# One block from the convolution to the ffn, with single waits in place of two block ends

## The reference

```python
mod = silu(c) @ w_ada + b_ada                      # sh1, sc1, g1, sh2, sc2, g2
h = x * (1 + sc1) + sh1
z, xbc, dt_raw, q, k, v, f_raw = split(h @ w_in)
xbc = silu(causal_depthwise_conv(xbc, conv_w, conv_b))
y_ssm = rms_norm((ssd_chunked(xs, dt, A, Bm, Cm) + d_skip * xs) * silu(z))
y_att = rms_norm(forgetting_attention(q, k, v, log_f))
x = layer_norm(ALPHA * x + (1 + g1) * (concat(y_ssm, y_att) @ w_out))
h = x * (1 + sc2) + sh2
x = layer_norm(ALPHA * x + (1 + g2) * (square(relu(h @ w_ff_in)) @ w_ff_out))
```

## Time and profile before

| what | us |
|---|---|
| median of 3 runs (2339.7 to 2341.65) | 2341.12 |
| profiled execution | 2340.7 |
| its span, first to last instruction | 2338.9 |
| TensorE busy | 2243.1 |
| VectorE busy | 869.9 |
| ScalarE busy | 646.1 |
| GpSimd busy | 335.7 |

### The profile page before, as it was taken

How to read it: one execution, slowest core, us unless ns; L and a number is a source line. 1 busy time by engine, 2 the same in 40 slices (tenths; PEclk the granted TensorE clock), 3 DMA queues, 4 the chain that set the end, 5 groups by cost and what they waited for, 6 DMA issues and landing times. The chain is left out here.

```text
span 2338.9 us, 27117 instructions
## 1 busy us (share of the span) xinstructions
PE 2243.1 (96%) x9635; PEld 1068.9 (46%) x9636; DVE 869.9 (37%) x1582; ACT 646.1 (28%) x850; POOL 335.7 (14%) x289
## 2 busy tenths in 40 slices
PE   6998999999799999989898999999999999999997
PEld 2444665644657567535545333333333333333332
DVE  1882666633535365533534122111112111111126
ACT  1211223221010000002300543434343443444430
POOL 4461114440000000001200011010001000010112
PEclk8999999999899999999895999999999999999999
DMA  8463323302623121141007969999999999999997
GB/s 327 189 210 88 82 54 108 135 18 72 234 78 136 75 72 72 55 163 39 1 27 312 377 270 393 421 423 405 424 423 411 422 409 423 422 408 423 422 414 300
DMA packets 139445, 569.43 MB, mean 243 GB/s; under 512 B 12311, under 2 KB 47308, under 8 KB 88172
## 3 DMA queue, kind: packets, MB, share of 16 engines
q1 hardware_dynamic: 123584, 527.89, 57.0%
q0 software_dynamic: 6272, 20.62, 2.2%
q10 hardware_dynamic: 9516, 19.99, 2.2%
HBM read 544.53 MB, written 23.92 MB: 243 GB/s over the span
## 5 line engine op out<-in xcount | busy, mean ns | idle before, releaser
L2656 PE MATMUL banks<-expert_ring,slot_token_gate 128*64 128x512 f32 x2880 | 636.7, 594 | 5.4 <-DMA expert_ring<-in_w_up_dram 3.1
L2656 PEld LDWEIGHTS banks<-expert_ring,slot_token_gate 128*64 128x64 f32 x2880 | 202.3, 137 | 400.2 <-issue 387.0
L2592 ACT COPY expert_ring<-expert_ring 128x2048 f32 x176 | 324.5, 1896 | 75.6 <-DMA expert_ring<-in_w_gate_dram 64.2
L2656 PE MATMUL banks<-expert_ring,slot_xT_gate 128*64 128x512 f32 x1440 | 329.8, 600 | 1.7 <-issue 1.0
L2656 PEld LDWEIGHTS banks<-expert_ring,slot_xT_gate 128*64 128x64 f32 x1440 | 100.6, 138 | 189.3 <-issue 181.9
L2769 DVE TENSOR_SCALAR col_onehot<-banks,slot_gates 128x512 f32<-128x512 f32 x45 | 33.8, 750 | 402.8 <-PE banks L2656 402.7
L521 PE MATMUL banks<-hT,weight_ring 128*128 128x512 f32 x320 | 142.6, 605 | 3.6 <-DMA weight_ring<-in_w_in_dram 2.7
L2754 DVE TENSOR_TENSOR slot_token_gate<-banks,expert_bias_T 128x512 f32<-128x512 f32 x45 | 31.1, 691 | 297.4 <-PE banks L2626 296.4
L2512 POOL COPY slot_ids<-slot_tokens 128x1 int32 (+1 forms) x45 | 8.2, 183 | 891.7 <-PE banks L2626 891.7
L1511 PE MATMUL banks<-hT,weight_ring 128*128 128x256 f32 x512 | 114.5, 384 | 6.6 <-PEq L2878 5.7
L1054 PE MATMUL banks<-hT,weight_ring 128*128 128x512 f32 x256 | 116.1, 604 | 0.0
(11 more groups left out here) (454 smaller groups left out, 2570.3 us busy)
## 6 DMA issues: line engine op xcount, KB each, us to landing
expert_ring<-in_w_gate_dram SPq DMA_DIRECT2D x128, 1024.0 KB, 14.8
expert_ring<-in_w_up_dram SPq DMA_DIRECT2D x128, 1024.0 KB, 13.2
expert_ring<-in_w_down_dram SPq DMA_DIRECT2D x128, 1024.0 KB, 11.8
weight_ring<-in_w_ada_dram SPq DMA_DIRECT2D x12, 2048.0 KB, 11.9
weight_ring<-in_w_in_dram SPq DMA_DIRECT2D x8, 2048.0 KB, 12.1
weight_ring<-in_w_ff_in_dram SPq DMA_DIRECT2D x8, 2048.0 KB, 11.0
weight_ring<-in_w_ff_out_dram SPq DMA_DIRECT2D x8, 2048.0 KB, 10.6
weight_ring<-in_w_in_dram SPq DMA_DIRECT2D x24, 512.0 KB, 5.9
```

Of the source, the lines that this page charges most:

```text
L2592: nc.scalar.copy(flat_ring[:, c * size:(c + 1) * size], flat_ring[:, bass.ds(source + c * size, size)])\
L2656: x = nc.tensor.matmul(ps[h * CAP:(h + 1) * CAP, bank, :], lhs[:, k % 4, (k // 4) * CAP:(k // 4 + 1) * CAP], X.ring[:, m, k, h * HALF:(h + ...
```

## The change

`stage_streams`, `stage_mixer` and `stage_ffn` share one block. Their tiles still take each other's place in memory, so where a block end stood, single waits stand on the readers of what is overwritten: the stream stage hands on four semaphores (`stream_read`, `silu_done`, `gates_read`, `mod2_ok`), the output projection its own. The semaphores of the three stages are cleared together, behind the ffn. In detail:

- SyncE stores the running sums before the last z load, not at the stage's end, and leaves the fourth head pair's load to the mixer.
- In the mixer's last step the square sums move behind two turns and a logits product, their mean on VectorE in front of the last turn but one and the last softmax.
- `att` takes a half and a range of depth. The transposes of tile 2 stand inside the last half of tile 3.
- P1 and P2 of the first ffn product form `first_products`: 40 records of P1 and P2, the transposes of tile 3, the other 24 records of P2, and then the waits on the last copies.
- SyncE's gain rows and GpSimd's zeros for the ffn wait for the last output product; ScalarE's program keeps its order.

```diff
@@ -383,15 +383,16 @@
-        block = ctx.enter_context(nc.Block())
+        G.stream_read, G.silu_done, G.gates_read, G.mod2_ok = f_read, acc_free, g_all, gstep
+        block = G.block
         @block.sync
         def _(sp):
-            G.W.upto(sp, G.W.index[("qkv", 0)] + RING)
-
+            G.W.upto(sp, G.W.index[("z", 1)])
             sp.wait_ge(rows_ok, 2)
             sp.dma_start(G.sums_dram[0:16, :], rows[0:16, :]).then_inc(G.sums_out, 16)
             sp.dma_start(G.sums_dram[16:32, :], rows[32:48, :]).then_inc(G.sums_out, 16)
+            G.W.upto(sp, G.W.index[("qkv", 0)] + RING - 1)
...
@@ -771,15 +772,14 @@
-        if h == 1:
+        if h == 1 and KB - 1 in depth:
...
-    def att(self, pe, t):
-        for h in range(2):
-            self.half(pe, t, h, KB, self.ATT[t][h], range(KB), self.y_done)
+    def att(self, pe, t, h, depth=range(KB)):
+        self.half(pe, t, h, KB, self.ATT[t][h], depth, self.y_done)
...
         nc.tensor.nop().then_inc(G.W.used, 2)
...
+        self.att(pe, 2, 0)
+        self.att(pe, 2, 1)
+        self.turn_x(pe, 1)
         pe.wait_ge(self.y_read, 1)
-        self.att(pe, 3)
+        self.att(pe, 3, 0)
+        self.att(pe, 3, 1, range(0, KB // 2))
+        self.turn_x(pe, 2)
+        self.att(pe, 3, 1, range(KB // 2, KB))
         pe.wait_ge(self.y_done, T)
         nc.tensor.nop().then_inc(G.W.used, 2)
-        turn_x(2)
-        turn_x(3)
...
@@ -909,11 +915,14 @@
-        block = ctx.enter_context(nc.Block())
+        G.out = out
+        block = G.block
 
         @block.sync
         def _(sp):
             sp.wait_ge(G.sums_out, 32)
+            sp.wait_ge(G.gates_read, 4)
+            sp.wait_ge(G.mod2_ok, 2)
...
@@ -1000,6 +1009,8 @@
+            act.wait_ge(G.gates_read, 4)
+            act.wait_ge(G.mod2_ok, 2)
...
+            pe.wait_ge(G.silu_done, XB)
+            pe.wait_ge(G.mod2_ok, 2)
             ssm_in(0)
+            pe.wait_ge(G.stream_read, XB + KB)
...
@@ -1160,8 +1174,6 @@
                     out.ssm(pe, 0, 1)
-                    pe.wait_ge(q["y_read"], PAIRS)
-                    out.square_sums(pe, 0)
                 if old:
                     turn(U + 2)
                     turn(U + 3)
@@ -1170,6 +1182,8 @@
                 else:
+                    pe.wait_ge(q["y_read"], PAIRS)
+                    out.square_sums(pe, 0)
                     pe.wait_ge(q["state_ready"], PAIRS)
                     out.ssm(pe, 1, 0)
...
+            dve.wait_ge(G.gates_read, 4)
...
@@ -1306,11 +1321,11 @@
                     softmax(U + 4)
                 if new:
                     ssm_out(j)
+                else:
+                    out.mean_square(dve, 0)
                 if old:
                     turned(U + 4)
                     softmax(U + 6)
-                    if not new:
-                        out.mean_square(dve, 0)
                     turned(U + 6)
...
@@ -1418,12 +1434,14 @@
 
         @block.sync
         def _(sp):
+            sp.wait_ge(out.y_done, T)
             ln.load(sp)
             G.W.upto(sp, G.W.index[("q2",)] + RING)
             sp.wait_ge(G.y_zeroed, 16 * (-(-(LIST - EXPERTS) * CAP // P)))
 
         @block.gpsimd
         def _(pool):
+            pool.wait_ge(out.y_done, T)
             nc.gpsimd.memset(zeros[:], 0.0).then_inc(zeros_ok, 1)
 
...
+            def up_block(f, name, j, b):
+                x, y = x_operand(f, seven.X_OF[name]), y_operand(f, seven.Y_OF[name])
+                at = (2 * j + b) * P
+                for k in range(4):
+                    m = nc.tensor.matmul(bank(f, name, j)[:, b, :], y[:, k, at:at + P], x[:, k, :],
+                                         start=(k == 0), stop=(k == 3))
+                if b:
+                    m.then_inc(seven.done, 1)
+
...
+            def first_products():
+
+                G.W.wait(pe, ("up", 0, 0))
+                pe.wait_ge(out.h_ok, 2 * KB)
+                pe.wait_ge(out.y_read, 3)
+                for j in range(2):
+                    for b in range(2):
+                        up_block(0, "P1", j, b)
+                up_block(0, "P2", 0, 0)
+                out.turn_x(pe, T - 1)
+                up_block(0, "P2", 0, 1)
+                for b in range(2):
+                    up_block(0, "P2", 1, b)
+                pe.wait_ge(out.y_read, T)
+                pe.wait_ge(out.h_ok, T * KB)
+
             def seven_products(f):
-                for name in seven.ORDER:
+                for name in seven.ORDER[2:] if f == 0 else seven.ORDER:
                     operands_ready(f, name)
-                    x, y = x_operand(f, seven.X_OF[name]), y_operand(f, seven.Y_OF[name])
...
+            first_products()
             for f in range(LAST):
                 seven_products(f)
             last_down()
...
+            dve.wait_ge(out.h_ok, T * KB)
             s_sums(0, G.hT)
...
+def stage_streams_to_ffn(nc, A, G):
+
+    with ExitStack() as ctx:
+        G.block = ctx.enter_context(nc.Block())
+        stage_streams(nc, A, G)
+        stage_mixer(nc, A, G)
+        G.mixer_tiles.close()
+        stage_ffn(nc, A, G)
+
...
@@ -2893,23 +2947,19 @@
...
-                    run_stage(nc, A, G, stage_prepare)
-                    run_stage(nc, A, G, stage_streams)
-                    G.X = ctx.enter_context(nc.sbuf_tensor("X", [P, T, D], F32, side="right"))
-                    run_stage(nc, A, G, stage_mixer)
-                mixed.close()
-                run_stage(nc, A, G, stage_ffn)
...
+                run_stage(nc, A, G, stage_prepare)
+                G.X = ctx.enter_context(nc.sbuf_tensor("X", [P, T, D], F32, side="right"))
+                run_stage(nc, A, G, stage_streams_to_ffn)
```

More of the change, by code:

```diff
@@ L789, in square_sums, with turn_x @@
         x.then_inc(self.ss_done, 1)
+    def turn_x(self, pe, t):
+        G = self.G
+        pe.wait_ge(self.ln.ready, t + 1)
+        if t:
+            pe.wait_ge(self.h_ok, KB * t)
+        for k in range(KB):
+            m = self.nc.tensor.transpose(G.ps[:, self.TURN[k // 4], (k % 4) * P:(k % 4 + 1) * P], G.X[:, t, k * P:(k + 1) * P],
+                                         G.ident[:])
+        m.then_inc(self.turned, 1)
     def rest(self, pe):
         nc, G = self.nc, self.G
[L795 to L802, removed]
         pe.wait_ge(self.a_done, T)
@@ L1383, in stage_ffn @@
         ln = Norm(nc, ctx, G, "ln2", A["ln2_g"][0:1, :], A["ln2_b"][0:1, :])
-        block = ctx.enter_context(nc.Block())
+        out = G.out
+        block = G.block
         def x_quarter(src):
@@ new lines, in down_block @@
+            def down_block(f, name, j):
+                x, y = x_operand(f, seven.X_OF[name]), y_operand(f, seven.Y_OF[name])
+                for k in range(4):
+                    m = nc.tensor.matmul(bank(f, name, j), x[:, k, j * P:(j + 1) * P], y[:, k, :],
+                                         start=(k == 0), stop=(k == 3))
+                m.then_inc(seven.done, 1)
+            def first_products():
[12 more added lines that the diff above has]
+                pe.wait_ge(out.h_ok, T * KB)
@@ L1496, in seven_products @@
             def seven_products(f):
-                for name in seven.ORDER:
+                for name in seven.ORDER[2:] if f == 0 else seven.ORDER:
                     operands_ready(f, name)
-                    x, y = x_operand(f, seven.X_OF[name]), y_operand(f, seven.Y_OF[name])
                     for j in range(2):
                         bank_ready(f, name, j)
-                        out = bank(f, name, j)
                         if f % 2:
-                            for k in range(4):
-                                m = nc.tensor.matmul(out, x[:, k, j * P:(j + 1) * P], y[:, k, :],
-                                                     start=(k == 0), stop=(k == 3))
+                            down_block(f, name, j)
@@ L1507, in seven_products @@
                         else:
                             for b in range(2):
[L1509 to L1513, removed]
+                                up_block(f, name, j, b)
                 pe.wait_ge(seven.done, 14 * (f + 1))
@@ L2895, in build @@
                 G.gate = sbc(gates, "gates", [P, 2, D])
-                mixed = ExitStack()
-                G.mixT = sbc(mixed, "mixT", [P, 2 * KB, S])
-                with ExitStack() as m:
-                    G.xbcT = sbc(m, "xbcT", [P, XB, S])
-                    G.w_dtf = sbc(m, "w_dtf", [P, KB, 32])
-                    G.head_rows = sbc(m, "head_rows", [P, 48])
-                    G.d_col = sbc(m, "d_col", [P, KB])
-                    G.dt = sbc(m, "dt", [P, T, 16])
-                    G.av = sbc(m, "rates", [P, T, 32])
-                    G.acs = sbc(m, "acs", [P, 64])
-                    G.decays = sbc(m, "decays", [P, 128])
-                    run_stage(nc, A, G, stage_prepare)
-                    run_stage(nc, A, G, stage_streams)
-                    G.X = ctx.enter_context(nc.sbuf_tensor("X", [P, T, D], F32, side="right"))
```

(16 more changed lines are left out.)

10 lines of the change are left out of this document (5 added, 5 removed).

## The result

| what | us |
|---|---|
| median after, 4 runs (2310.86 to 2317.26) | 2312.11 |
| median before beside them, 4 runs (2335.32 to 2341.65) | 2340.41 |
| ratio after to before, 95% interval | 0.9888 [0.9869, 0.9906] |
| profiled execution after, its span | 2317.26, 2315.4 |

The change is faster by 1.1%, about 26 us (22 to 31 by the interval); forecast were 13.6. Two later series gave 0.9904 and 0.9908, 22 us.

What follows compares the result with a forecast made beforehand. TensorE was taken as the bound, so gains come from its idle time at two stage boundaries and the mixer's last step: 8.8 + 4.5 + 5.2 - 4.9 = 13.6 us off 2340.7, forecast 2327, range 2319 to 2334.

Steps and rivals of the forecast that it cites:

- First boundary: Z stage to mixer: the mixer's transposes start without the block end's wait and the score tile is ready; 8.8 us gained.
- Mixer's last step: End of the mixer: the reordered square sums and their mean remove TensorE's waits of 1.14 and 3.42 us; 4.5 us gained.
- Second boundary, P1 to P3: Last norm and ffn: first ffn products fill the norm, P3 starts at 602.4 after 1.2 idle; 13.3 us so far.
- Second boundary, P6: Ffn: the zero fill's 19.4 us issue on ScalarE delays P6's operand sum; TensorE idles 6.3 us, net gain 5.2.
- Clearing: Behind the ffn: 82 semaphore clears moved there at 60 ns each, with TensorE idle; 4.9 us lost.
- the first one: Ffn: the zero fill doesn't hold P6, so 13.3 us are kept; 21.7 us gained in all, 2319; chance 0.07.
- a stretched fill: Ffn: each zero-fill store takes twice its time, P6 starts 12.3 us later than before; 2347, slower; chance 0.03.
- The other two: First boundary gives nothing, 2336, chance 0.07; clock after P6's idle time and clears cost 2.6 us more, 2330, chance 0.13.

Runs made afterwards that it cites:

- e1: The changed kernel with ScalarE's zero fill held back until SyncE's down weights and gains have landed; 0.9984 of the kernel before.
- e4: The kernel before with only the streams and the mixer put in one block, with waits on single readers; 0.9976 of the kernel before.
- e7: The changed kernel with the semaphores of the streams and the mixer cleared by SyncE under the ffn's products; 0.9906 and 0.9904 of the kernel before.
- e8: The changed kernel with the zero fill in 32 stores of half the size instead of 16; its one execution took 2345.23 us.
- b1: The kernel before, unchanged, profiled a second time; the zero fill's issue took 18.13 us.
- b2: The kernel before, unchanged, profiled a third time; the zero fill's issue took 18.92 us.

## Why the prediction was wrong

- **First boundary**: right, 8.8. The transposes ran without a wait, the score tile was in time.
- **Mixer's last step**: right mechanism, short term. 4.9 against the profile that I forecast from, but 7.8 and 9.6 against two other executions of the kernel before, since the gaps usually cost clock as well. I had priced the clock at the two boundaries only.
- **Second boundary, P1 to P3**: right. From the last output product to P3 16.65 us (585.89 - 569.24) against a forecast 16.15, with the wait of 1.4 for the half sum.
- **Second boundary, P6**: this step failed: "so I take the row's 19.4 unchanged". The issue took 12.9 in the new place. I had the weights through by the fill's start, and 3.5 us of them were still to come; that this made the issue short fits e1 (18.2 behind landed loads), but e4 had 12.4 in the old place, so what sets the length stays open in part. It also began with the first of ScalarE's last copies and not behind them, 1.5 us earlier. With 19.4 the sum would have ended at 604.2, 4.4 us late, or 5.9 with the later start, near the 6.3 that I had. As it was, it ended 2.07 early, and with no idle time no clock was lost: 13.2 instead of 5.2. In e1 the long issue comes back and holds P6.
- **Clearing**: right, 4.9, and e7 takes it back.
- **Rivals**: the first one, that the fill doesn't hold P6, came true: 21.7 by its sum, 22.0 in the traces. Its reason, stores issued as fast as the first ones of a queue, held for the first nine only (0.39 to 0.65 us each; the last seven took 0.89 to 1.75). I gave it 0.07 because the DMA engines were full, which they were: a full engine says how fast stores move, not how far their issue may run ahead. The second, a stretched fill, didn't occur here, but e8 shows that it can. The other two fell.

The first rival's 2319 is the lower end of the range. The profiled execution after, 2317.26, lies 1.7 below it, the median of 2312.11 some 7. One profile as the base explains it in part: from the start of the last z product to P6 the kernel before took 629.47 - 182.46 = 447.0 us in it, but 632.59 - 180.93 = 451.7 in b1 and 631.42 - 179.35 = 452.1 in b2, the changed kernel 599.78 - 179.68 = 420.1. Less the 4.9 of the clears that is 22 us saved against the first and 27 against the other two, most of the difference by the clock in the mixer's last step. The rest is what executions differ by, as in the second stage's clock, and isn't told apart here.

One reading of the earlier trace rows was wrong: three of the forty slices lie under eight tenths, the last one too; no term rests on it.

## What to carry to other kernels

The length of a run of DMA issues is not a property of the instruction: before carrying it to a new place, ask what its queue will find in the engines there, and keep both its shortest rows and the pace of the movement as bounds for whatever stands behind it on its engine. A small wait on TensorE can cost as much in clock as in idle time (4.7 and 4.6 us in b2), and not in every execution: price it from a second one. Clears that a merged block moves behind its end are a loss of 60 ns each that a queue with slack can do earlier.

## What the runs showed of the hardware

- Stores from 64 partitions instead of 128 kept the DMA engines as busy (1.01 against 1.02) at 206 instead of 417 GB/s.
- Sixteen equal stores of 0.5 MB took ScalarE's queue from 12.4 to 21.8 us to issue, with landing times from 6.0 to 19.0 us. The Trainium skill ("Perfetto Trace Analysis", DMA Instruction — HWDGE (DVE, Sync)) says that the time shown for a DMA instruction covers the generation of its descriptors and the push of its semaphore, not the movement of the data, and its drawing has a DMA engine start early when a buffer is full. That the issue keeps the pace of the movement in e1 agrees with such a buffer; a fixed size of it is not seen.
- A gap of 3.42 us on TensorE left the product behind it at 7.13 us in one execution and stretched it to 10.02 and 10.20 us in two others of the same program, with a granted clock of 1.00 and of 0.84 and 0.88 from 490 to 505 us.
